# Spare TensorE matmuls on constants inside its waits, and latent sums behind a weight chunk, in a two-block transformer kernel

## The chip, the cores and the metric

One core of a Trainium2 chip runs the whole program. The metric is the device time of one execution in microseconds, lower is better. Engines are named as the profile names them: PE is TensorE's matmuls, PEld its weight loads, DVE VectorE, ACT ScalarE, POOL GpSimd and SP SyncE.

## What is computed

512 tokens of width 1024, all in 32-bit floats, go through two transformer blocks. The first has three branches (windowed attention, a spatial gate, a pooling branch) that are gated and merged, an attention on 256 memory tokens, and a feed-forward layer. The second has two causal attentions over 512 tokens (MLA with a low-rank latent, and "fox" with forget gates) and a layer of experts in which every token takes 16 of 16384 experts in each of 8 heads:

```python
x = x + rmsnorm(merged @ w_out[l], g_norm[l, 1])
ym = memory_attention(rmsnorm(x, g_norm[l, 2]), rmsnorm(mem, g_mem[l]), ...)
x = x + rmsnorm(ym, g_norm[l, 3])
yf = jnp.square(jax.nn.relu(rmsnorm(x, g_norm[l, 4]) @ w_up[l])) @ w_down[l]
x = x + rmsnorm(yf, g_norm[l, 5])
...
h = _modulate(x, norm1_g, shift1, scale1)
cq, ckv, kpe, fq, fk, fv, fl = split(h @ w_in)
q_a = _rms_norm(cq, mla_qa_g) @ w_uq;  kv_a = _rms_norm(ckv, mla_kva_g) @ w_ukv
x = x + gate1 * (concat(attention_a, attention_b) @ w_o)
h2 = _modulate(x, norm2_g, shift2, scale2)
# experts: 16 best of 256 candidate pairs per head; rows of peer_u and peer_v are gathered
a = einsum("bcd,bchkd->bchk", h2, peer_u[e]);  y = einsum("bchk,bchkd->bcd", gate * gelu(a), peer_v[e])
```

## The kernel before

The tokens are done in two halves of 256 (`TH` = 2 tiles of 128; `W` = 256). For each half, `dense(hf)` runs all layers on TensorE, with the activations feature-major: a linear layer is a stream of 128x256 matmuls, eight for each weight chunk of 512 KB. SP loads the chunks in one fixed order into a ring of five; `take` waits for one. Results go to four PSUM banks in turn: `bank()` waits until the result of four banks ago has been emptied (semaphore `lin_evacuated`) and hands out the next one, `lin[0]` counts them.

Each engine has a program of its own, whose order is fixed when the kernel is built. The expert work of half 0 (gathers of `peer_u` rows and dot products on VectorE, then gathers of `peer_v` rows and batches of 16 matmul records in `combine`, L897) is woven into half 1's dense work by a pace that is worked out at build time: `fill()` and `tick()` place the batches that are due by the program's own clock. Half 1's experts come at the end, with nothing dense beside them. In half 0 there is no expert work, and `fill()` places nothing.

Places that the change touches, in the order of a half:

- `attend` (L832): an attention as a pipeline of steps. A step makes the scores of unit i (L846), transposes the probabilities of unit i-2 (L855) and multiplies those of i-3 with the values (L864). The band, memory, mla and fox attentions take 8, 4, 8 and 8 heads by two tiles. At the first head of a tile the output bank must be free (`o_normed` of an earlier group). At a tile's end TensorE waits for the normalised output `o_normed`, transposes it (L872), and the attention ends with a wait for the last copy `pt_copied`. `turned_room` waits until a transposition bank is free. In half 0 other matmuls are put between the steps (gate weights, modulation, fox keys, output weights).
- `sums_of_added` and `sums` (L709, L722): square sums over the features as matmuls against a column of ones (L717, L730), followed by ScalarE's root and VectorE's reciprocal; `spread` (L735) waits for them and spreads the factor over the partitions (L741). `norm` (L744) is both. It is called for the first and second residual norm of half 1 and for the last (`z3`) of both.
- the first norm of the second block: `sums(KB, each=2)`, `spread(True)`, then `linear_fm(hT, 5)` (cq, ckv), a narrow `linear_tok(hT, 1, 40)`, the latent square sums `sums(3)` and `sums(2, first=3)`, then the four chunks of fox values with a `spread()` after the second and the fourth.
- the end of half 0's dense work: `sums(KB, sq=sq_next)` for the next half's first norm, then transposes of h2 (L1210).

## Time and profile before

| | us |
|---|---|
| median of 3 runs (lowest to highest) | 2486.91 (2478.14 to 2488.8) |
| profiled execution, its time | 2490.19 |
| profiled execution, span of its instructions | 2488.4 |
| TensorE busy | 1954.1 (79%) |
| VectorE, ScalarE, GpSimd busy | 1232.9, 503.6, 1098.6 |

### The profile page before, as it was taken

What the parts mean: (1) busy time and instruction counts of PE and PEld (TensorE: products, weight loads), DVE (VectorE), ACT (ScalarE), POOL (GpSimd) and SP (SyncE); (2) the same over time, 40 slices, a digit from 0 to 9 for tenths busy, and PEclk for the clock granted to TensorE, in tenths of its full rate; (3) what the DMA queues carried; (4) which work ended last, traced back from release to release, by engine and by line L of the source; (5) the groups of instructions that cost most, each with busy time, mean ns of one, the idle gap of its engine ahead of it and who ended that gap; (6) DMA issues with size and microseconds to landing.
All of it is one profiled execution on the core that took longest, in us unless ns stands there. A gap on an engine that the chain in (4) does not pass through costs nothing.

```text
span 2488.4 us, 26319 instructions
## 1 busy us (share of the span) xinstructions
PE 1954.1 (79%) x9392; PEld 1363.5 (55%) x9392; DVE 1232.9 (50%) x2969; ACT 503.6 (20%) x1204; POOL 1098.6 (44%) x1090
## 2 busy tenths in 40 slices
PE   8999999999989989998999999887933333333334
PEld 6888778887557767776777764553810000000001
DVE  5455120002425876547634447664667666666540
ACT  3411331101442232124211022442110000000000
POOL 2010000000001556455555554675577777777764
PEclk9999999998989999999999989799956566556557
DMA  7486324443416999999999998899999999999997
GB/s 282 170 318 252 123 94 153 153 152 102 145 55 237 396 354 385 394 405 356 393 389 405 388 360 334 308 353 368 352 362 411 409 409 409 409 410 409 409 409 315
DMA packets 214996, 780.06 MB, mean 313 GB/s; under 512 B 23923, under 2 KB 26547, under 8 KB 213843
## 3 DMA queue, kind: packets, MB, share of 16 engines
q0 software_dynamic: 155120, 564.84, 58.2%
q1 hardware_dynamic: 57560, 208.49, 23.2%
q10 hardware_dynamic: 2187, 5.05, 0.6%
q8 instruction: 76, 1.25, 0.2%
q14 instruction: 53, 0.43, 0.1%
HBM read 771.70 MB, written 6.58 MB: 313 GB/s over the span
## 4 chain that ended last, share of the span: by engine, by line
PE 64%; DMA 14%; POOL 10%; issue 5%; DVE 4%; ACT 3%; ACTq 0%; SPq 0%; POOLq 0%; DVEq 0%
PE bank L648 50%; POOL main L581 8%; DMA main<-in_peer_v,idx_v 6%; PE bank L912 5%; DMA main<-in_peer_u,idx 5%; DMA ring<-in_peer_u,idx 2%; PE bank L846 2%; PE bank L864 2%; POOL ring L581 1%; PE bank L855 1%; ACT main L1259 1%; DMA ring<-in_w_stream 1%; PE bank L730 1%; DVE main L1901 1%; PE bank L1227 1%
## 5 line engine op out<-in xcount | busy, mean ns | idle before, releaser
L648 PE MATMUL bank<-main,ring 128*128 128x256 f32 x4864 | 1078.9, 383 | 10.1 <-ACT main L1477 5.0
L648 PEld LDWEIGHTS bank<-main,ring 128*128 128x128 f32 x4864 | 923.3, 191 | 166.3 <-issue 34.1
L912 PE MATMUL bank<-main,w_wide 128*32 128x512 f32 x2048 | 354.0, 825 | 430.6 <-DMA main<-in_peer_v,idx_v 419.6
L581 POOL DMA_INDIRECT main<-in_peer_v,idx_v x512 | 525.2, 1026 | 371.6 <-PE bank L912 230.6
L581 POOL DMA_INDIRECT main<-in_peer_u,idx x427 | 456.0, 1068 | 268.2 <-issue 116.6
L912 PEld LDWEIGHTS bank<-main,w_wide 128*32 128x32 f32 x2048 | 71.6, 134 | 650.5 <-issue 649.5
L1901 DVE CUSTOM_DVE_ANT_0 main<-h_a,main 128x1024 f32<-128x1024 f32 x256 | 311.4, 1220 | 114.0 <-DMA main<-in_peer_u,idx 101.8
L1259 ACT ACTIVATE main<-bank 128x256 f32<-128x256 f32 (+3 forms) x304 | 125.0, 420 | 700.4 <-PE bank L648 681.4
L648 PE MATMUL bank<-ring,main 128*128 128x512 f32 (+3 forms) x624 | 238.2, 535 | 7.3 <-DMA ring<-in_w_stream 7.3
L1901 DVE CUSTOM_DVE_ANT_0 main<-bank,main 128x1024 f32<-128x1024 f32 x144 | 175.0, 1216 | 122.7 <-DMA main<-in_peer_u,idx 121.5
L648 PEld LDWEIGHTS bank<-ring,main 128*128 128x128 f32 x624 | 108.8, 195 | 109.7 <-issue 95.4
L576 POOL DMA_DIRECT2D main<-in_norm_g x1 | 0.5, 527 | 355.0 <-ACT small L1279 355.0
L1901 DVE CUSTOM_DVE_ANT_0 ring<-bank,ring 128x1024 f32<-128x1024 f32 x80 | 97.2, 1215 | 94.0 <-DMA ring<-in_peer_u,idx 93.5
L574 POOL DMA_DIRECT2D main<-in_w_ada x48 | 25.3, 528 | 190.3 <-DVE main L1757 190.3
L1721 DVE TENSOR_TENSOR main<-main 128x256 f32<-128x256 f32 x36 | 15.3, 424 | 181.0 <-ACT main L1469 180.9
L846 PE MATMUL bank<-main 128*128 128x256 f32 (+9 forms) x224 | 85.9, 471 | 13.6 <-ACT main L1338 7.9
L864 PE MATMUL bank<-main 128*128 128x64 f32 (+1 forms) x496 | 80.8, 296 | 19.0 <-ACT main L1352 11.5
L581 POOL DMA_INDIRECT ring<-in_peer_u,idx x85 | 80.1, 943 | 25.9 <-issue 24.1
L864 PEld LDWEIGHTS bank<-main 128*128 128x128 f32 x496 | 73.2, 215 | 27.1 <-ACT main L1352 21.8
L1374 ACT ACTIVATE dots<-dots 128x32 f32<-128x32 f32 x16 | 3.7, 229 | 415.0 <-DVE dots L1901 415.0
L1338 ACT ACTIVATE main<-bank,small 128x256 f32<-128x256 f32 (+3 forms) x112 | 57.1, 510 | 140.4 <-DVE small L1783 85.8
L1469 ACT ACTIVATE main<-bank 128x256 f32<-128x256 f32 x48 | 18.4, 383 | 279.7 <-PE bank L648 279.7
(247 smaller groups left out, 1512.0 us busy)
## 6 DMA issues: line engine op xcount, KB each, us to landing
ring<-in_w_stream SPq DMA_DIRECT2D x372, 512.0 KB, 6.2
main<-in_w_ada POOLq DMA_DIRECT2D x48, 512.0 KB, 9.7
main<-in_peer_v,idx_v POOLq DMA_INDIRECT x512, 11.3
main<-in_peer_u,idx POOLq DMA_INDIRECT x427, 10.6
main<-in_sub_keys SPq DMA_DIRECT2D x2, 1024.0 KB, 9.8
main<-rows_d SPq DMA_DIRECT2D x1, 1536.0 KB, 10.5
ring<-in_peer_u,idx POOLq DMA_INDIRECT x85, 17.2
main<-in_xT ACTq DMA_DIRECT2D x1, 1024.0 KB, 5.3
```

Of the source, the lines that this page charges most:

```text
L574: gp.dma_start(ada_ring[:, p % ADA_RING, :], T["w_ada"][k * P:(k + 1) * P, s * D:(s + 1) * D]).then_inc(ada_landed[p % ADA_RING], 16)
L581: gp.indirect_dma_start(rows_buf[slot], None, table, bass.IndirectOffsetOnAxis(ap=where, axis=0)).then_inc(landed[slot], 16)
L648: ins = pe.matmul(o, lhsT, rhs, **kw)
L730: last = mm(b[:, t:t + 1], sq[:, first + k, t * P:(t + 1) * P], ones[:, 0:1], start=k == 0 and t == 0, stop=k == nb - 1, skip_group_check= ...
L846: mm(s_bank[u % 2][:, 0:nk], q_of(x), k_of(x, b0 * P, nk), start=True, stop=True).then_inc(S["s_ready"], 1)
L855: last = pe.transpose(pt_bank[x["r"] % 2][:, j * P:(j + 1) * P], probs[:, u % 3, j * P:(j + 1) * P], ident)
L864: last = mm(o_bank(x)[:, x["h"] * dv:(x["h"] + 1) * dv], probsT[:, u % 2, j * P:(j + 1) * P], v_of(x, kb_), start=j == 0, stop=j == len(x[ ...
L912: last = mm(y_bank[half][s * CG:(s + 1) * CG, :], w_wide[:, lo:lo + CG], v_buf[slot][:, half * 512:(half + 1) * 512], start=q == 0, stop=q ...
L1227: last = mm(b[:, p * P:(p + 1) * P], qpT[:, (2 * h + p) % KB, t * P:(t + 1) * P], sub_keys[:, 2 * h + p, :], start=True, stop=True)
L1259: ac.activation(dst, s, func, **kw).then_inc(S["lin_evacuated"], 1)
L1338: ac.activation(probs[:, u % 3, 0:nk], s_bank[u % 2][:, 0:nk], ACT.Exp, scale=neg_r[:, x["tl"]:x["tl"] + 1] if kind == "mem" else -1.0, bi ...
L1901: st.begin(ve.tensor_tensor_reduce(out=u_buf[slot], in0=h2, in1=u_buf[slot], scale=1.0, scalar=0.0, op0=ALU.mult, op1=ALU.add, accum_out=d ...
```

## The change

`keep_busy(n, bank)` issues n matmuls of the identity with 256 constant columns into a PSUM bank that is free at that time; nothing reads the result. `keep_busy_dense(n)` does so in the bank that `bank()` would give next, after the same wait. They are called:

- in `sums_of_added` ahead of the wait for the squares (1, in `norm`), in `sums` for every second block (1), in `spread(True)` ahead of the wait for the factor (2) and behind it (4 in `norm`, 2 in the second block's norm), the last two only where `fill()` places no expert batch; `fill()` now returns whether it did;
- in `attend` behind the second scores if no batch was placed there (3), ahead of the wait for the output bank at the second tile's first head where both tiles use the same bank (3), ahead of the wait for the last normalised output (2, with `turned_room` moved in front), and ahead of the last copy (1);
- at half 0's h2: 1 for every second of eight blocks of the sums, and 3 behind them.

The latent sums are moved behind the first of the four fox value chunks; their two banks and the two of the values are taken ahead of that chunk.

```diff
--- before.py
+++ after.py
@@ -629,6 +629,7 @@
             lin = [0]
             clock = [0.0]
             experts_now = [None]
+            batches = [0]
 
             mm = pe.matmul
 
@@ -641,8 +642,21 @@
 
             def fill():
 
+                placed = batches[0]
                 if experts_now[0] is not None:
                     experts_now[0].until(clock[0] + EARLY)
+                return batches[0] > placed
+
+            def keep_busy(n, idle_bank):
+
+                for _ in range(n):
+                    mm(idle_bank[:, 0:W], ident, cst[:, 0:W], start=True, stop=True)
+
+            def keep_busy_dense(n):
+
+                if n and lin[0] > 3:
+                    pe.wait_ge(S["lin_evacuated"], lin[0] - 3)
+                keep_busy(n, psum[lin[0] % 4])
 
             def mmw(o, lhsT, rhs, **kw):
                 ins = pe.matmul(o, lhsT, rhs, **kw)
@@ -706,9 +720,10 @@
             norms = [0]
             sq_seen = [0]
 
-            def sums_of_added(hf, name, b=None):
+            def sums_of_added(hf, name, b=None, busy=0):
 
                 b = bank() if b is None else b
+                keep_busy(busy, b)
                 n, other = (KB, KB - 1) if name[0] == "z" else (KB // 2, 1)
                 pe.wait_ge(S["sq_ready"], SQUARES[hf][name] + n)
                 pe.wait_ge(S["sq_added"], ADDED[hf, name])
@@ -719,12 +734,14 @@
                 sq_seen[0] += n
                 results(last)
 
-            def sums(nb, first=0, sq=sqT, b=None, each=1):
+            def sums(nb, first=0, sq=sqT, b=None, each=1, busy=0):
 
                 b = bank() if b is None else b
                 for k in range(nb):
                     if k % each == 0:
                         sq_seen[0] += 1
+                    if k % 2 == 0:
+                        keep_busy_dense(busy)
                     pe.wait_ge(S["sq_ready"], sq_seen[0])
                     for t in range(TH):
                         last = mm(b[:, t:t + 1], sq[:, first + k, t * P:(t + 1) * P], ones[:, 0:1],
@@ -734,8 +751,8 @@
             def spread(may_fill=False, r=rstd):
 
                 norms[0] += 1
-                if may_fill:
-                    fill()
+                if may_fill and not fill():
+                    keep_busy_dense(2)
                 pe.wait_ge(S["rstd_ready"], norms[0])
                 for t in range(TH):
                     last = mm(rbc[:, t * P:(t + 1) * P], r[:, t:t + 1].to_broadcast([P, P]), ident, start=True, stop=True)
@@ -743,10 +760,11 @@
 
             def norm(hf, name):
 
-                sums_of_added(hf, name)
+                sums_of_added(hf, name, busy=1)
                 spread(True)
                 clock[0] += 6.0
-                fill()
+                if not fill():
+                    keep_busy_dense(4)
 
             def mod_row(s):
 
@@ -844,8 +862,9 @@
                             pe.wait_ge(S["p_ready"], u - 1)
                         b0, nk = x["blocks"][0], len(x["blocks"]) * P
                         mm(s_bank[u % 2][:, 0:nk], q_of(x), k_of(x, b0 * P, nk), start=True, stop=True).then_inc(S["s_ready"], 1)
-                        if i == 1:
-                            fill()
+                        if i == 1 and not fill():
+                            turned_room(units[0]["r"])
+                            keep_busy(3, pt_bank[units[0]["r"] % 2])
                     if 2 <= i <= n + 1:
                         x = units[i - 2]
                         u = x["u"]
@@ -859,6 +878,8 @@
                         u = x["u"]
                         pe.wait_ge(S["pt_copied"], x["r"] + 1)
                         if x["h"] == 0 and x["g_prev"] is not None:
+                            if x["tl"] and not x["other"]:
+                                keep_busy(3, pt_bank[x["r"] % 2])
                             pe.wait_ge(S["o_normed"], x["g_prev"] + 1)
                         for j, kb_ in enumerate(x["blocks"]):
                             last = mm(o_bank(x)[:, x["h"] * dv:(x["h"] + 1) * dv], probsT[:, u % 2, j * P:(j + 1) * P],
@@ -866,15 +887,20 @@
                         last.then_inc(S["av_done"], 1)
                     if i in ends:
                         x = ends[i]
+                        turned_room(x["ro"])
+                        if i == max(ends):
+                            keep_busy(2, pt_bank[x["ro"] % 2])
                         pe.wait_ge(S["o_normed"], x["g"] + 1)
-                        turned_room(x["ro"])
                         for j in range(4):
                             last = pe.transpose(pt_bank[x["ro"] % 2][:, j * P:(j + 1) * P], o_tok[:, j * P:(j + 1) * P], ident)
                         last.then_inc(S["pt_ready"], 1)
                     while early is not None and early_done < by_step(total, steps, i):
                         early_done = next(early)
                     tick(each)
-                pe.wait_ge(S["pt_copied"], ends[max(ends)]["ro"] + 1)
+                last_ro = ends[max(ends)]["ro"]
+                pe.wait_ge(S["pt_copied"], last_ro)
+                keep_busy(1, pt_bank[(last_ro + 1) % 2])
+                pe.wait_ge(S["pt_copied"], last_ro + 1)
 
             def turn_idx(k):
 
@@ -896,6 +922,7 @@
 
             def combine(b):
 
+                batches[0] += 1
                 for s in range(N_CG):
                     slot, fills = v_slot(N_CG * b + s)
                     pe.wait_ge(v_landed[slot], 16 * (fills + 1))
@@ -1059,17 +1086,20 @@
                     results(last)
                 mark("norm3")
                 norm(hf, "z3")
-                sums(KB, each=2)
+                sums(KB, each=2, busy=1)
                 spread(True)
                 clock[0] += 6.0
-                fill()
+                if not fill():
+                    keep_busy_dense(2)
                 mark("cq")
                 linear_fm(hT, 5, first_wait=h_block)
                 linear_tok(hT, 1, 40)
-                sums(3)
-                sums(2, first=3)
+                q_sums, kv_sums = bank(), bank()
                 banks = [bank() for _ in range(TH)]
-                tok_chunks(banks, hT, 0, 2, 4, 512)
+                tok_chunks(banks, hT, 0, 1, 4, 512)
+                sums(3, b=q_sums)
+                sums(2, first=3, b=kv_sums)
+                tok_chunks(banks, hT, 1, 2, 4, 512)
                 spread()
                 results(tok_chunks(banks, hT, 2, 4, 4, 512), TH)
                 spread()
@@ -1199,7 +1229,8 @@
                         tick(7.1)
                 mark("h2")
                 if hf == 0:
-                    sums(KB, sq=sq_next)
+                    sums(KB, sq=sq_next, busy=1)
+                    keep_busy_dense(3)
                 clock[0] += 6.0
                 fill()
                 for t in range(TH):
```

## Rows read from the trace of the kernel before

**Rows 1.** The page's granted clock in tenths, in 40 equal slices of 62 us.
```profile
PEclk9999999998989999999999989799956566556557
```

**Rows 2.** Stages: from:to length, busy PE PEld DVE ACT POOL, clock, DMA share, GB/s.
```profile
0.00:815.00 815.00, 773.01 (x3498) 625.41 (x3499) 253.91 (x574) 222.60 (x561) 49.54 (x79) 0.96 0.50 173
815.00:1445.00 630.00, 608.23 (x3111) 475.33 (x3110) 371.53 (x934) 138.26 (x348) 358.94 (x322) 0.99 0.99 387
1445.00:1740.00 295.00, 262.49 (x1263) 154.44 (x1263) 178.32 (x396) 99.27 (x209) 168.75 (x150) 0.90 0.91 343
...
1815.00:2488.40 673.40, 240.20 (x1132) 52.83 (x1132) 383.10 (x926) 25.83 (x45) 482.74 (x504) 0.61 1.00 397
```

**Rows 3.** Stretches of low granted clock, same columns.
```profile
113.10:116.50 3.40, 3.27 (x15) 3.27 (x16) 1.42 (x4) 1.15 (x4) 0.00 (x0) 0.50 0.01 2
...
300.90:314.50 13.60, 13.60 (x55) 12.17 (x55) 2.70 (x10) 5.13 (x16) 0.00 (x0) 0.50 0.00 1
...
573.90:587.60 13.70, 11.24 (x43) 10.36 (x44) 8.19 (x17) 6.21 (x13) 0.53 (x1) 0.50 0.17 52
608.10:614.90 6.80, 6.80 (x17) 4.13 (x17) 0.17 (x1) 0.52 (x2) 0.00 (x0) 0.50 0.22 69
693.40:703.60 10.20, 8.32 (x37) 6.98 (x38) 2.65 (x5) 4.98 (x9) 0.00 (x0) 0.50 0.00 0
...
741.20:744.60 3.40, 3.40 (x15) 2.99 (x14) 0.00 (x0) 2.29 (x4) 0.20 (x1) 0.50 0.02 4
765.10:775.30 10.20, 6.94 (x26) 5.89 (x25) 5.70 (x12) 3.76 (x8) 0.00 (x0) 0.50 0.06 9
...
1126.90:1130.30 3.40, 3.39 (x8) 2.76 (x9) 3.23 (x6) 3.37 (x8) 1.37 (x2) 0.50 1.03 410
...
1488.70:1492.10 3.40, 3.40 (x6) 1.32 (x5) 0.00 (x0) 1.32 (x2) 0.07 (x1) 0.50 1.03 410
1574.00:1594.50 20.50, 20.50 (x74) 13.42 (x74) 10.75 (x30) 6.42 (x18) 12.16 (x11) 0.50 0.90 332
1601.30:1611.60 10.30, 9.72 (x34) 7.47 (x35) 3.97 (x12) 2.75 (x8) 1.68 (x2) 0.50 0.63 232
```

**Rows 4.** PE's timeline, waits in brackets: start, busy, line, tiles, form, count.
```profile
111.89 0.66 PE L872 MATMUL bank<-cst,main 128*128 128x128 f32 x4 [1.28 <-DVE main L1797]
...
299.43 0.61 PE L788 MATMUL bank<-ones,main 128*128 128x1 f32 x4 [1.96 <-ACT gate L1299]
...
574.46 6.96 PE L730 MATMUL bank<-ones,main 128*128 128x1 f32 x32 [2.33 <-ACT main L1478]
...
582.04 1.22 PE L741 MATMUL bank<-cst,small 128*128 128x128 f32 x4 [0.62 <-DVE small L1697]
...
710.05 0.49 PE L846 MATMUL bank<-main 66*128 66x128 f32 x2 [2.02 <-ACT main L1338]
...
1601.88 1.94 PE L864 MATMUL bank<-main 128*128 128x64 f32 x8 [2.15 <-DVE main L1797]
```

**Rows 5.** The chain that ended last: start, length, engine, line, records.
```profile
805.23 6.91 PE bank L648 x32
...
1590.68 3.57 PE bank L912 x16
...
1612.44 1.85 PE bank L912 x16
```

**Rows 6.** PE's timeline where a spare would meet little or no wait.
```profile
76.72 1.46 PE L648 MATMUL bank<-main,ring 128*128 128x256 f32 x6
...
1186.49 0.71 PE L741 MATMUL bank<-cst,small 128*128 128x128 f32 x4 [0.55 <-DVE small L1697]
...
1624.88 0.66 PE L872 MATMUL bank<-cst,main 128*128 128x128 f32 x4
```

**Rows 7.** PE's waits 1560 to 1740 us (total, times, longest), and a POOL timeline row.
```profile
PE bank L912 <- DMA main<-in_peer_v,idx_v: 17.1, 6, 5.5
...
1612.98 1.25 POOL L581 DMA_INDIRECT main<-in_peer_u,idx  x1 [8.38 <-DVE dots L1901]
```

## The prediction

> **What bounds the kernel now.** I read the granted clock of the page first, then the busy time by stage, then TensorE's timeline around each place where the clock is low, then the waits of the gathers. The clock line [rows 1] is at or near full for most slices and dips at a few of the first 29. Every dip that I enlarged is a stretch at 0.50 exactly, which is the 1.2 GHz level against 2.4 GHz. By stage [rows 2], tokens of half 0 (0 to 815 us) and half 1 (815 to 1740) keep TensorE busy 95%, 97% and 89% of the time: there TensorE is the bound. From 1815 us on it is 36% busy and the DMA engines are full at 397 GB/s: that end is a queue of gathered expert rows, its length set by bytes. It starts when the routing of half 1 is through, so a microsecond saved before about 1740 us should be a microsecond off the end. TensorE's slow clock in the end stretch costs nothing.
>
> The mean clocks of the first three stages (0.96, 0.99, 0.90) mean 2 x (0.04 x 815 + 0.01 x 630 + 0.10 x 295) = 137 us at half speed before 1740 us. At most half of that, 68 us, can come back, and only where TensorE is what the stretch waits for. This is the ceiling.
>
> **What precedes a dip.** It is waiting of one or two microseconds, not long idleness: the end of the first attention (1.28 us for the normalised output) is followed by 1.2 GHz, so are the head of the memory attention (1.96), the fox head (2.02) and the last norm of the first block (2.33) [rows 4]. The length of the low stretch is out of proportion to the wait: 13.6 us after 1.96 [rows 3].
>
> **Price of a spare.** 32 records, which are 16 matmuls of 128x256, take 6.91 us [rows 5]: 0.43 us for one. An expert batch takes 1.85 us at 2.4 GHz and 3.57 at 1.2 [rows 5], so a spare that runs at the low level is 0.83.
>
> **Part 1, spares at the ends of attentions** (two ahead of the wait for the normalised output, one ahead of the last copy). 0.86 us lies in waits like the 1.28 of the first attention; hidden. Four stretches of 3.4 us in half 0 hang on an end or on the fox head; the first and the last of them have TensorE busy 3.27 and 3.40 us [rows 3]. That is dense work at half speed, so about 1.6 each; at the fox head each unit also waits for ScalarE, so I take 1.4 as the mean: **5.6 us**. The mla end (10.2 us low, 8.3 busy [rows 3]) begins ahead of the spares; they can only bring the clock back sooner. Between 0 and 3; I take 1.5.
>
> **Part 2, three spares at the heads**, 1.3 us, placed only if no expert batch was placed there. In the memory attention of half 0 they fit the wait of 1.96 [rows 4]. The 13.6 us behind it are wholly TensorE-busy [rows 3], on many small matmuls that cannot bring the clock back by themselves. Half of it is 6.8; I take **6.5**. In half 0's band attention the next matmuls follow the scores without a wait [rows 6], because chunks of gate weights are put there: three spares are 1.3 us on the path. The mla head has such fillers too; I charge both in full: **-2.6**.
>
> **Part 3, three spares ahead of the second tile's first output**, which must wait for the normalisation of the first tile (same PSUM bank): 1.3 in the 2.15 us of half 1's mla attention [rows 4]. The 10.3 us low behind it are 9.7 busy [rows 3]: **5.0**.
>
> **Part 4, the last norm of the first block and its square sums.** One spare, two, then four and one more in the waits up to 2.33 [rows 4]: hidden. In half 0 13.7 us are low with 11.2 busy [rows 3], but VectorE's and ScalarE's chain hides part of it. Of the sums, 8 records of one column for each pair of blocks run in the low stretch, and with the clock up TensorE no longer trails the squares. Against it stand four spares between the pairs, and two behind in a wait of 0.62 [rows 4], 0.24 too short for them. If the clock falls during the sums all the same, those spares cost double. Bounds -3 and +3.5; I take **2** because the first wait is well filled.
>
> **Part 5, latent sums behind one chunk of weights.** Single-column sums right behind a narrow matmul are followed by 6.8 us low, all busy [rows 3]: half, 3.4, is the most. But all four banks are now taken ahead of the chunk, so TensorE first waits until ScalarE has emptied the last narrow results, and the narrow matmul is itself light work, so the fall may come anyway. 0 to 3.4; **1.5**. SP's weight queue keeps its order; no DMA is moved. The sums end one chunk later, and one chunk instead of two stands between them and their use.
>
> **Part 6, h2 of half 0**: seven spares (3.0 us) around sums that run without a wait, ahead of transposes that wait for VectorE; 10.2 us low with 6.9 busy [rows 3]. Hidden only because the second tile's rows come late. If not hidden, -3; **2.1** taken: the dense part of the stretch at half price.
>
> Half 0: 5.6 + 1.5 + 6.5 - 2.6 + 2 + 1.5 + 2.1 = 16.6 us.
>
> **Half 1.** The same sites gain less, as expert batches fill or occupy the waits. Four low stretches at norms and latent sums, the first and last 3.4 us [rows 3], together 3.1: there VectorE and ScalarE pace the blocks. The mla second tile: 5.0. Exposed spares: two behind a batch at the mla end, where the transposes now follow at once [rows 6], two likewise at the band end, three at the second norm against a wait of 0.55 [rows 6], one at the fox end: 0.86 + 0.86 + 0.74 + 0.43 = 2.9. Net 5.2. The largest stretch, 20.5 us low and wholly busy at 1574 [rows 3], is not in the sum: a batch is placed at that head, so no spare is.
>
> **Sum**: 16.6 + 5.2 = 21.8 us. The profiled execution took 2490.2 us, 3.3 above the median of 2486.9; the slow stretches differ from run to run as waits fall differently, so I subtract from the median: **2465 us**. 0.5% (12.4 us) is about what a measurement of this kernel can tell from no change.
>
> **A rule against it.** The Trainium skill (TensorE: Matmul & The Clock Gate, Why this matters for your kernels) warns of idle gaps between bursts of matmuls that are longer than any wait filled here. By it these waits would not lower the clock, and the spares could give nothing. The trace disagrees in the four places of [rows 4] named above. The rival that it makes is the second below.
>
> **Rivals.**
> *The mla head of half 1 stays fast too.* It began after several short waits, and its matmuls then held a pace at 1.2 GHz that never brought the clock back. A small shift in what precedes could spare it. About 7.5 of 20.5 us, as at full clock the units are bound by VectorE and ScalarE: 2457. For: the start moves. Against: no spare is put there. 0.20.
> *Spares do not move the clock.* The waits are a symptom, and the light work around them (transposes, single columns) is what lowers it. Then only exposed spares count: 2.6 + 2.9, some 6 us: 2493. Against: dense work ends each low stretch. 0.08.
> *Half 1's gain is taken back by gathers.* TensorE already waits 17.1 us for value rows between 1560 and 1740 us [rows 7]; a faster TensorE asks for them sooner. For: these waits. Against: GpSimd itself sat 8.4 us waiting for a VectorE dot just ahead of that [rows 7], and that dot is held up by the slow stretch at 1601. Half 0's gain alone: 2470. 0.12.
> *The dips move.* Waits that stay unfilled, such as those ahead of the mla attentions, catch the clock where they missed it before, and half the gain goes: 2476. 0.09.
> *Slower: spares at the low level.* Where the clock has fallen before the spares, they run at 0.83 each and push the awaited transposes and sums back. If they restored it nowhere: about 0.7 for each of eight attention ends (three spares are 2.5 us there, of which I estimate that waits like the 1.28 [rows 4] hide two thirds), 4 for the sums of each half's last norm, 1 for h2 beyond its wait, with 2.6 + 2.9 doubled: 5.6 + 8 + 1 + 11 = 26 us, less waits that hide a third: about 18: 2505. It decides against the kernel from the point where over half the sites are already low when the spares start. For: the mla end and the band end of half 1. Against: elsewhere the wait itself is the first lapse. 0.06.
>
> **How the numbers follow.** Forecast 0.45, with 2456 to 2474 of its own from parts 4 to 6. The range leaves out the second and last rival and a tail of the first: 2447 to 2483. Faster by over 0.5% (below 2474.5): forecast 0.44, first rival 0.20, third 0.09, fourth 0.04, so 0.77. Slower (above 2499.3): 0.05. Within: 0.18.
>
> **What would show it.** Right: the granted clock at 1.00 through the memory attention of half 0, at both its ends and at the second mla tile of half 1; TensorE's waits there filled by the new matmul line; batches and the end queue unchanged in length. Wrong: low stretches of the same length after filled waits (second rival); longer waits of TensorE for value rows between 1560 and 1740 (third); a spare line with a mean near twice 0.43 us and waits gone ahead of it (last); or low clock at 655 to 660 us or around 900, where it was full before (fourth).

## The result, and the profile after

The median of 18 executions went from 2491.04 to 2477.82 us; the ratio is 0.9946 (95% interval 0.9927 to 0.9965), some 13.4 us less. The forecast was 21.8 us less. So the time fell, as forecast, and lies within the range, by about three fifths of the expected amount. The kernel before came out 4.1 us above the 2486.91 that the forecast started from; the rest of the distance from 2465 to 2477.8 is a gain that was forecast too large. The profiled execution took 2483.59 us, 5.8 above the median (its span 2481.8), which matters below: it holds a long stretch at 1.2 GHz that some other profiles lack.

The granted clock on the page of after, beside [rows 1]:

```profile
PEclk9999999998999999999999999979965566565556
```

Stages of after (from:to length, busy time and records of PE, PEld, DVE, ACT, POOL, granted clock, DMA share, GB/s). In order: half 0's memory attention with its output layer; half 0's last norm of the first block to the end of the fox values; the same of half 1; half 1's mla attention; its fox attention; the end stretch.

```profile
295.10:331.10 36.00, 33.58 (x184) 27.49 (x185) 8.96 (x26) 16.62 (x46) 0.00 (x0) 1.00 0.19 59
562.40:650.00 87.60, 86.63 (x321) 56.27 (x321) 33.02 (x80) 26.33 (x52) 0.53 (x1) 0.90 0.36 118
...
1440.00:1546.10 106.10, 103.64 (x442) 58.45 (x443) 70.33 (x161) 30.42 (x58) 48.23 (x46) 1.00 0.93 351
1554.20:1605.30 51.10, 46.04 (x285) 29.25 (x286) 43.73 (x111) 22.90 (x55) 41.12 (x33) 0.97 0.99 368
1605.30:1675.60 70.30, 64.92 (x338) 42.40 (x339) 36.82 (x79) 26.30 (x62) 41.07 (x39) 0.76 0.81 291
1797.70:2481.80 684.10, 252.24 (x1171) 54.89 (x1169) 388.10 (x942) 31.40 (x54) 489.72 (x508) 0.58 1.00 395
```

The memory attention is now wholly at 2.4 GHz. The fox attention of half 1 is at 0.76, where before it was at 0.94 and the mla attention at 0.76: the long low stretch of half 1 [rows 3, the one at 1574] has not gone; in this profile it stands one attention later. The end stretch is as long as it was (682.3 before, 684.1 now, both from the last key score to the end of the span), so of the 8.4 us that the dense part gains in these two profiles all but 1.8 reach the end.

The same stages in both kernels and in four experiments told below, in us, each from its first matmul to the next stage's first; in brackets the us at 1.2 GHz, where there are any, summed from the granted clock (0.3 us and less, and the end, are left out):

| stage | before | after | no spares | half 0 spares | half 1 spares | first units |
|---|---|---|---|---|---|---|
| half 0 band attention | 37.9 | 39.2 | 38.0 | 39.2 | 38.0 | 37.9 |
| to the memory attention | 181.4 (3.3) | 179.8 | 181.4 (3.4) | 179.8 | 181.3 (3.1) | 179.8 |
| half 0 memory attention | 43.2 (17.1) | 36.0 | 40.4 (10.2) | 36.0 | 44.9 (20.5) | 36.0 |
| half 0 last norm to fox values | 86.3 (20.5) | 87.6 (17.1) | 85.4 (17.1) | 84.5 (10.2) | 84.6 (17.1) | 85.9 (13.7) |
| half 0 mla attention | 35.4 (6.3) | 35.6 (3.1) | 35.5 (2.4) | 35.2 | 35.5 (6.5) | 35.6 (3.1) |
| half 0 fox attention | 41.1 (7.4) | 39.8 (3.7) | 44.6 (14.6) | 38.9 | 41.1 (7.2) | 39.8 (3.7) |
| half 0 output layer, h2 | 40.8 (13.6) | 39.4 (3.4) | 40.9 (13.6) | 39.2 (6.8) | 40.7 (13.7) | 39.5 (3.4) |
| half 1 mla attention | 63.2 (30.7) | 51.0 (3.4) | 54.0 (10.2) | 51.9 (6.8) | 50.9 (3.4) | 50.0 |
| half 1 fox attention | 56.6 (6.8) | 70.4 (34.1) | 67.6 (30.7) | 58.2 (6.8) | 70.1 (34.1) | 56.2 |
| last key score to last matmul | 675.9 | 677.3 | 675.5 | 675.6 | 677.7 | 675.8 |

The waits that were filled, in TensorE's timeline of after (start, busy, line, tiles, form, count, wait ahead): the end of the first attention, the head of the memory attention, and the fox head of half 0, as three of [rows 4]. L653 is a spare, L895 the transposes of a finished output, L806 the woven modulation.

```profile
112.45 1.08 PE L653 MATMUL bank<-cst 128*128 128x256 f32 x4
113.90 0.66 PE L895 MATMUL bank<-cst,main 128*128 128x128 f32 x4 [0.36 <-DVE main L1828]
...
297.75 1.46 PE L653 MATMUL bank<-cst 128*128 128x256 f32 x6
299.87 0.61 PE L806 MATMUL bank<-ones,main 128*128 128x1 f32 x4 [0.66 <-ACT gate L1330]
...
700.13 0.71 PE L864 MATMUL bank<-main 66*128 66x128 f32 x4 [1.67 <-ACT main L1290]
700.68 1.80 PE L653 MATMUL bank<-cst 128*128 128x256 f32 x6
```

The wait of 1.28 is 0.36 now, that of 1.96 is 0.66. At the fox head the spares stand behind the scores, while the wait is ahead of them: 1.67 of 2.02 us is left, and 3.7 us stay at the low level in that attention.

### The profile page after: what moved, and what is told of

The parts are those of the page before. It is cut to its first block, busy times and chain, and to the rows that moved or that the text cites. A ratio compares the mean times of both kernels' runs of the same rounds, so it can differ in the third digit from the quotient of the medians.

```text
span 2481.8 us, 26696 instructions
## 1 busy us (share of the span) xinstructions
PE 1983.9 (80%) x9588; PEld 1374.1 (55%) x9588; DVE 1231.7 (50%) x2969; ACT 503.2 (20%) x1204; POOL 1098.7 (44%) x1090
## 3 DMA queue, kind: packets, MB, share of 16 engines
q8 instruction: 78, 1.28, 0.2%
## 4 chain that ended last, share of the span: by engine, by line
PE 60%; DMA 15%; POOL 12%; issue 6%; DVE 4%; ACT 3%; SPq 0%; POOLq 0%; DVEq 0%; ACTq 0%
PE bank L662 48%; POOL main L581 11%; DMA main<-in_peer_v,idx_v 5%; DMA main<-in_peer_u,idx 5%; PE bank L939 4%; DMA ring<-in_peer_u,idx 3%; PE bank L864 2%; PE bank L885 1%; POOL ring L581 1%; PE bank L653 1%; DVE main L1932 1%; DMA ring<-in_w_stream 1%; ACT main L1290 1%; PE bank L874 1%; PE bank L1258 1%
## 5 line engine op out<-in xcount | busy, mean ns | idle before, releaser
L939 PE MATMUL bank<-main,w_wide 128*32 128x512 f32 x2048 | 361.7, 841 | 425.8 <-DMA main<-in_peer_v,idx_v 414.8
L939 PEld LDWEIGHTS bank<-main,w_wide 128*32 128x32 f32 x2048 | 72.1, 135 | 651.8 <-issue 650.6
L885 PE MATMUL bank<-main 128*128 128x64 f32 (+1 forms) x496 | 77.2, 286 | 13.2 <-ACT main L1383 12.6
L864 PE MATMUL bank<-main 128*128 128x256 f32 (+9 forms) x224 | 82.1, 452 | 6.7 <-ACT main L1290 5.0
L1369 ACT ACTIVATE main<-bank,small 128x256 f32<-128x256 f32 (+3 forms) x112 | 57.2, 511 | 137.5 <-DVE small L1814 87.6
L885 PEld LDWEIGHTS bank<-main 128*128 128x128 f32 x496 | 69.2, 204 | 22.7 <-ACT main L1383 19.9
L1814 DVE CUSTOM_DVE_ANT_0 bank<-bank,cst 128x128 f32<-128x128 f32 (+3 forms) x64 | 31.9, 498 | 86.8 <-PE bank L864 86.7
## 6 DMA issues: line engine op xcount, KB each, us to landing
main<-in_peer_u,idx POOLq DMA_INDIRECT x427, 10.3
```

What stands on the lines that cost most here:

```text
L864: mm(s_bank[u % 2][:, 0:nk], q_of(x), k_of(x, b0 * P, nk), start=True, stop=True).then_inc(S["s_ready"], 1)
L885: last = mm(o_bank(x)[:, x["h"] * dv:(x["h"] + 1) * dv], probsT[:, u % 2, j * P:(j + 1) * P], v_of(x, kb_), start=j == 0, stop=j == len(x[ ...
L939: last = mm(y_bank[half][s * CG:(s + 1) * CG, :], w_wide[:, lo:lo + CG], v_buf[slot][:, half * 512:(half + 1) * 512], start=q == 0, stop=q ...
L1369: ac.activation(probs[:, u % 3, 0:nk], s_bank[u % 2][:, 0:nk], ACT.Exp, scale=neg_r[:, x["tl"]:x["tl"] + 1] if kind == "mem" else -1.0, bi ...
L1814: st(ve.tensor_tensor_reduce(out=s[:, 0:nk], in0=s[:, 0:nk], in1=causal, scale=1.0, scalar=3.0e38, op0=ALU.add, op1=ALU.min, accum_out=low ...
```

## The experiments

The theory: a short wait of TensorE is followed by a stretch at 1.2 GHz, and spare work in the wait prevents it. The rivals: the clock does not follow the spares; the gain is handed back to the experts' gathers; half 1's long stretch comes and goes by itself.

**Spares without columns.** All spares keep their places and count, but stream one column instead of 256.

```diff
-mm(idle_bank[:, 0:W], ident, cst[:, 0:W], start=True, stop=True)
+mm(idle_bank[:, 0:1], ident, cst[:, 0:1], start=True, stop=True)
```

> The changed kernel with every spare cut from 256 columns to one: same count, places and waits, nearly no work in them. If the spares act by the work that they give TensorE (my theory), the granted clock falls again at the head of half 0's memory attention, some 13 us at 0.50, and the time is that of the kernel before, ratio 0.999 to 1.003. If it is enough that TensorE issues something in the wait, or if the gain came from the moved waits and the moved sums, the ratio stays near 0.9946.

Measured: 2497.66 us, ratio 1.0038 (1.0018 to 1.0058). The memory attention of half 0 in a window (columns as above):

```profile
295.70:335.70 40.00, 36.47 (x185) 31.25 (x184) 8.96 (x26) 16.73 (x45) 0.00 (x0) 0.87 0.17 53
```

and in TensorE's timeline:

```profile
298.93 0.72 PE L653 MATMUL bank<-cst 128*128 128x1 f32 x6
301.05 0.61 PE L806 MATMUL bank<-ones,main 128*128 128x1 f32 x4 [1.39 <-ACT gate L1330]
```

A wait of 1.39 us is left, and the clock falls (0.87; 36.0 us and 1.00 in after). The time is a little above the range that was expected for this theory. So the work in the spares carries the whole gain. It doesn't tell whether it is the columns or the time that they fill: the light spares do less of both. This kernel's ratio is above that of one without spares (below), though their intervals overlap; its profiled execution was its fastest (2484.98 us) and shows little of it, so whether it is slower, and why, is open.

**Spares in the batch's wait at two heads of half 1.** In after, a head at which an expert batch is placed gets no spares, even where TensorE then waits inside the batch for value rows. Here 4 (mla) and 10 (fox) spares stand ahead of that wait.

```diff
+HEAD_SPARES = {"mla": 4, "fox": 10}
...
+if i == 1 and hf and kind in HEAD_SPARES:
+    turned_room(units[0]["r"])
+    head_busy[0] = (HEAD_SPARES[kind], pt_bank[units[0]["r"] % 2])
...
 batches[0] += 1
+if head_busy[0] is not None:
+    keep_busy(*head_busy[0])
+    head_busy[0] = None
```

> The changed kernel with spares also in half 1's wait for value rows at the heads of the mla attention (4) and the fox attention (10), between the expert weights' turn and the batch. Theory: the changed kernel's 34 us at 0.50 in half 1's fox attention follow from that unfilled wait; filled, the stretch stays at 1.00, fox is some 13 us shorter than in the changed kernel's profile, and the median gains 4 to 10 us more, ratio to before 0.990 to 0.993. Rival: the gathers set the pace there, so TensorE waits longer for value rows later and the ratio stays at 0.9946.

Measured: 2475.74 us, ratio 0.9949 (0.9928 to 0.9969), no different from after. But its two attentions, mla and fox, are at full clock from end to end, the first kernel of which that is true; their windows:

```profile
1553.70:1604.50 50.80, 46.46 (x292) 30.56 (x292) 43.59 (x111) 22.92 (x55) 40.87 (x33) 1.00 1.00 369
1604.50:1659.80 55.30, 54.20 (x359) 37.15 (x360) 36.64 (x79) 26.31 (x62) 44.19 (x37) 1.00 0.96 351
```

and its fox head in TensorE's timeline (L654 spares, L950 a batch):

```profile
1611.75 4.48 PE L654 MATMUL bank<-cst 128*128 128x256 f32 x20
1616.64 1.92 PE L950 MATMUL bank<-main,w_wide 128*32 128x512 f32 x16 [0.41 <-DMA main<-in_peer_v,idx_v]
```

The two attentions take 106.1 us, against 121.4 in after. The expected ratio (0.990 to 0.993) didn't come: the median doesn't show what the profile shows. So what one profile shows here is probably not what every execution does. The later kernels take this up.

**The latent sums back in front.**

```diff
-q_sums, kv_sums = bank(), bank()
-banks = [bank() for _ in range(TH)]
-tok_chunks(banks, hT, 0, 1, 4, 512)
-sums(3, b=q_sums)
-sums(2, first=3, b=kv_sums)
-tok_chunks(banks, hT, 1, 2, 4, 512)
+sums(3)
+sums(2, first=3)
+banks = [bank() for _ in range(TH)]
+tok_chunks(banks, hT, 0, 2, 4, 512)
```

> The changed kernel with the latent sums back in front of the fox value chunks. In the profiles the stretch from the narrow matmul to the turn of the mla keys took 54.2 us after the change against 52.1 before. If the move costs, the ratio falls to 0.993 to 0.9945 and one wait of about 0.6 us ahead of the first value chunk goes; if it gains as I forecast (1.5 us in half 0, less in half 1), the ratio rises to 0.9955.

Measured: 2479.91 us, ratio 0.9976 (0.9954 to 0.9998), in the same comparison as the heads kernel. The intervals overlap, so the move's own worth isn't settled, though the ratio lies on the side on which the move gains, above the 0.9955 expected of that. In half 0 the stage from the last norm to the fox values is 85.4 us here and 81.7 to 87.6 in the eight profiles with both the move and half 0's spares there.

**Three spares at one head alone**, that of half 0's memory attention, in the kernel before.

```diff
 if i == 1:
     fill()
+    if kind == "mem" and not hf:
+        turned_room(units[0]["r"])
+        for _ in range(3):
+            mm(pt_bank[units[0]["r"] % 2][:, 0:W], ident, cst[:, 0:W], start=True, stop=True)
```

> The kernel before with one part alone: three spares behind the second scores of half 0's memory attention. Theory: the low stretch of 13.6 us there is gone, the stage from its first score to the second norm's sums is 36 instead of 43 us, and the time falls by 5 to 7 us, ratio 0.997 to 0.998. Rival: half 1 gives it back at its waits for expert rows, ratio 1.000 with the stage shorter all the same.

Measured: 2478.23 us, ratio 0.9983 (0.9958 to 1.0008). The median can't tell 4 us from nothing; the stage can:

```profile
295.40:331.40 36.00, 32.30 (x178) 26.61 (x178) 8.96 (x26) 16.57 (x46) 0.00 (x0) 1.00 0.18 59
```

43.2 us became 36.0, and the 17.1 us at 1.2 GHz are gone, for 1.3 us of spares. One wait of 1.96 us was the cause of all of it, the 3.4 us at the end of that attention (321.3 to 324.7 us in the kernel before) included, where this kernel has no spare. It is no chance of one profile: the stage takes 36.0 or 36.1 us, without low clock, in all ten profiles that have these spares, and 40.0 to 44.9 in the four that have none or light ones. The rule that the prediction weighed (the Trainium skill, TensorE: Matmul & The Clock Gate, Why this matters for your kernels), that the gaps which cost are longer ones, does not hold here: an edit shows it, not only the order in time.

**The moves without spares** (`keep_busy` issues nothing), **the spares of half 0 only, those of half 1 only, and all of them once more**, beside one another on one chip. In the first three the latent sums are where after has them.

```diff
 def keep_busy(n, idle_bank):
-    for _ in range(n):
-        mm(idle_bank[:, 0:W], ident, cst[:, 0:W], start=True, stop=True)
+    if experts_now[0] is None:      # half 0 only; "is not None": half 1 only; no spares: pass
+        for _ in range(n):
+            mm(idle_bank[:, 0:W], ident, cst[:, 0:W], start=True, stop=True)
```

> The changed kernel without any spare: only the latent sums behind the first value chunk and the waits that were moved forward are left. If the spares carry the whole gain, the ratio to before is 0.999 to 1.002. If the moved parts cost something of their own, as the run with one-column spares suggests (1.0038), it is 1.002 to 1.004. If the latent move gains by itself, 0.997 to 0.999.

> The changed kernel with the spares of half 0 alone, the moves kept in both halves. By my sum half 0 carries 16.6 of 21.8 us, so about three quarters of the gain: ratio 0.995 to 0.9965. If the exposed spares of half 1 eat what the others win there, it equals the whole change, 0.9946, or is better.

> The changed kernel with the spares of half 1 alone, the moves kept. By my sum 5 us, ratio 0.998 to 0.999. If half 1's gain is given back at the waits for value rows, or its exposed spares eat it, 1.000 to 1.002 (as e5_no_spares).

> The changed kernel itself, on the same chip as the three parts: 0.9946 again. Its profile shows whether the 34 us at 0.50 in half 1's fox attention come back: if they follow from that head's wait for value rows in every execution, they are there again; if it is chance how the waits fall, this profile is without them.

| spares | median us | ratio | interval |
|---|---|---|---|
| none | 2490.44 | 1.0004 | 0.9980 to 1.0028 |
| half 0 | 2478.95 | 0.9970 | 0.9946 to 0.9995 |
| half 1 | 2490.06 | 1.0017 | 0.9997 to 1.0038 |
| both | 2477.49 | 0.9961 | 0.9941 to 0.9981 |

The last row is after itself, which gave 0.9946 in the first comparison: a gain of 10 us here, of 13 there. As far as these intervals tell, the whole gain is half 0's. Half 1's spares give nothing that can be measured, and the moves alone nothing; the 0.998 to 0.999 that was expected of half 1 lies outside its interval. In the profile of half 1's spares the long stretch stands in the fox attention, as in after and in the kernel with no spares; with all spares a second time it stands in the mla attention, as in before. So which of the two attentions has the stretch in after is hardly an effect of the change.

**What holds the stretch.** TensorE's timeline of after at half 1's fox head (L939 is an expert batch of 16 records, L864 scores, L874 transposes, L885 the products with the values):

```profile
1608.95 1.92 PE L939 MATMUL bank<-main,w_wide 128*32 128x512 f32 x16
...
1617.86 3.64 PE L939 MATMUL bank<-main,w_wide 128*32 128x512 f32 x16 [5.22 <-DMA main<-in_peer_v,idx_v]
...
1629.81 1.59 PE L864 MATMUL bank<-main 66*128 66x384 f32 x2
1631.19 0.85 PE L874 MATMUL bank<-cst,main 128*128 128x128 f32 x3
1631.83 1.38 PE L885 MATMUL bank<-main 128*128 128x64 f32 x6
...
1646.80 3.64 PE L939 MATMUL bank<-main,w_wide 128*32 128x512 f32 x16
...
1651.41 0.60 PE L874 MATMUL bank<-cst,main 128*128 128x128 f32 x4
```

It begins with a wait of 5.22 us for value rows. Then each unit takes 3.2 us (1629.81 to 1633.01) and TensorE is busy all through, without leaving 1.2 GHz. The first dense work is the batch at 1646.80, and behind it the clock is full (transposes of four blocks in 0.60, of three in 0.85 ahead of it). In every profile with such a stretch and without a burst in it (before, after, no spares, half 1 spares, both again, lean) it ends with an experts' batch, or less than 1 us behind one. Three kernels test this.

**A burst.** After, with eight spares once in the eighth unit of half 1's mla and fox attention.

```diff
 turned_room(x["r"])
+if hf and kind in ("mla", "fox") and i == 7:
+    keep_busy(8, pt_bank[x["r"] % 2])
```

> The changed kernel with 8 more spares, once, in the eighth unit of half 1's mla and once of its fox attention. If the long low stretch of these attentions holds itself there, because their thin matmuls don't win the clock back once it has fallen, the burst ends it: no low stretch behind the eighth unit, at most some 15 us of low clock in either attention, and executions that lie closer together; it costs 3.4 us each (8 by 0.43) where the clock was full already, and saves up to 8 where it wasn't, so a ratio of 0.992 to 0.996. If the stretch comes from something outside TensorE, it runs past the burst (24 to 34 us of low clock in one of them), and the burst only costs: ratio 0.996 to 0.999.

Measured: 2481.46 us, ratio 0.9972 (0.9950 to 0.9993). Its long stretch was in the fox attention again; TensorE's timeline there (L653 spares, L864 scores, L876 transposes, L887 products):

```profile
1635.30 0.85 PE L876 MATMUL bank<-cst,main 128*128 128x128 f32 x3
1635.94 1.38 PE L887 MATMUL bank<-main 128*128 128x64 f32 x6
1637.11 1.59 PE L864 MATMUL bank<-main 66*128 66x384 f32 x2
1638.50 5.24 PE L653 MATMUL bank<-cst 128*128 128x256 f32 x16
1643.57 0.49 PE L876 MATMUL bank<-cst,main 128*128 128x128 f32 x3
1643.90 0.78 PE L887 MATMUL bank<-main 128*128 128x64 f32 x6
```

The same instructions take 0.85 and 1.38 ahead of the burst, 0.49 and 0.78 behind it: the clock comes back 3.3 us into the spares, where the units ahead of them had stayed low. Other thin work did win it back elsewhere: in the kernel before the low stretch that ends at 703.6 [rows 3] ends within a row of 32 transposes that began at 699.67. As an edit the burst doesn't pay: 20.6 us at 1.2 GHz had gone ahead of it and 3.3 more went in it, the fox attention is 69.5 us against 70.4, and the burst in the mla attention, where the clock was full, made it 53.6 instead of 51.0. The stretch ended in the burst, as expected of one that holds itself; the expected price (0.992 to 0.996) did not come out. The ratio lies where the rival, a cause outside TensorE, had it (0.996 to 0.999), but by that rival the stretch would have run past the burst.

**A lean kernel.** After, with the spares inside the two heads, and without those that its trace shows in full on the path (half 0's band head; the ends of half 1's band, mla and fox attention).

```diff
 if i == 1 and not placed:
     turned_room(units[0]["r"])
-    keep_busy(3, pt_bank[units[0]["r"] % 2])
+    if hf or kind != "band":
+        keep_busy(3, pt_bank[units[0]["r"] % 2])
...
-if i == max(ends):
+if i == max(ends) and (not hf or kind == "mem"):
     keep_busy(2, pt_bank[x["ro"] % 2])
...
-keep_busy(1, pt_bank[(last_ro + 1) % 2])
+if not hf or kind == "mem":
+    keep_busy(1, pt_bank[(last_ro + 1) % 2])
```

> The changed kernel, less the spares that its trace shows in full on the path (three at the head of half 0's band, and those at the ends of half 1's band, mla and fox attention, where an experts' batch stands ahead of them), and with 4 and 10 spares inside the batch's wait for its value rows at the heads of half 1's mla and fox attention. The theory that spares pay where they keep the clock and cost their own duration where nothing waits: band of half 0 back to 37.9 us (-1.3), band, mla and fox ends of half 1 each 1 to 2 us shorter, no long low stretch at either head; some 4 us below the changed kernel at least, ratio to the kernel before 0.990 to 0.993. The rival, that what half 1's dense work gains is given back to the experts' transfers: ratio 0.994 to 0.996, as the changed kernel.

> Both edits of the two kernels beside it. If the filled waits at the two heads already keep the clock, the bursts only cost: 6.8 us above the lean kernel, ratio 0.993 to 0.996. If the low stretch still comes back in part of the lean kernel's executions, the bursts save there what they cost elsewhere, and the two are within 2 us, with executions that lie closer together here.

Measured: lean 2473.96 us, ratio 0.9942 (0.9921 to 0.9962); with bursts too, 2474.21, 0.9957 (0.9936 to 0.9978). The lean kernel misses the expected 0.990 to 0.993; the two lie within 2 us of one another, as was expected if the stretch still comes back. The fox attention is at full clock in both profiles, as in the heads kernel, but the mla attention has the long stretch (20.5 and 17.1 us), although its head was filled. The lean kernel's window of the mla attention, and in TensorE's timeline the beginning and end of the stretch (L865 scores, L892 products with the values, L952 a batch):

```profile
1550.50:1609.10 58.60, 54.19 (x287) 35.55 (x288) 43.22 (x111) 22.88 (x55) 38.69 (x33) 0.83 0.88 321
```

```profile
1556.89 0.91 PE L865 MATMUL bank<-main 96*128 96x384 f32 x2 [0.59 <-ACT main L1382]
...
1559.26 0.91 PE L865 MATMUL bank<-main 96*128 96x384 f32 x2 [1.13 <-ACT main L1382]
...
1560.82 0.88 PE L892 MATMUL bank<-main 128*128 128x64 f32 x6 [0.32 <-ACT main L1396]
1561.54 1.51 PE L865 MATMUL bank<-main 96*128 96x384 f32 x2
1562.84 0.85 PE L881 MATMUL bank<-cst,main 128*128 128x128 f32 x3
...
1578.02 3.64 PE L952 MATMUL bank<-main,w_wide 128*32 128x512 f32 x16
```

It follows three waits of 0.59, 1.13 and 0.32 us for ScalarE in the first units, which no spare fills. Over all 14 profiles, two waits of 0.59 to 1.64 us, ahead of the third and the fourth score, stand in exactly the four that have the long stretch in the mla attention (before, both again, lean, lean with bursts). The heads kernel has one (1.10), the other nine none above 0.3. In eight of these nine the batch at that head waits 2.3 to 3.1 us for its rows; in the four it waits 1.6 us or less. So in this attention the long stretch goes with the shorter wait at the head, and filling that head alone left the next two waits open. In the kernel with bursts the eight spares stand at 1569.60, and the low stretch ends in them, at about 1572.

**The first units filled.** The lean kernel with two spares ahead of the third and two ahead of the fourth score of half 1's mla attention.

```diff
 if i < n:
     x = units[i]
     u = x["u"]
+    if hf and kind == "mla" and i in (2, 3):
+        keep_busy(2, pt_bank[units[i - 2]["r"] % 2])
     if u >= 2:
         pe.wait_ge(S["p_ready"], u - 1)
```

> The lean kernel with two more spares ahead of the third and two ahead of the fourth score of half 1's mla attention, where the traces show TensorE waiting 0.6 to 1.24 us for ScalarE's probabilities. If the long low stretch there (20.5 us in the lean kernel's profile, from its third unit on) begins in these short waits, it is gone: at most 6.8 us of low clock in the mla attention, 51 to 53 us instead of 58.5, a ratio of 0.990 to 0.993. If waits that short play no part, the stretch is there as before (17 us or more of low clock), and the ratio is that of the lean kernel or up to 0.0005 above it, 0.994 to 0.995. The four spares cost at most 1.7 us.

Measured: 2467.49 us, ratio 0.9932 (0.9905 to 0.9959), with six executions from 2464.54 to 2475.63. Its window of the mla attention, and its first units in TensorE's timeline (L654 spares, L867 scores):

```profile
1555.10:1605.10 50.00, 47.06 (x295) 30.76 (x296) 42.88 (x111) 22.84 (x55) 40.24 (x33) 1.00 1.00 368
```

```profile
1560.10 1.13 PE L654 MATMUL bank<-cst 128*128 128x256 f32 x4
1561.41 0.91 PE L867 MATMUL bank<-main 96*128 96x384 f32 x2 [0.18 <-ACT main L1384]
...
1562.49 1.03 PE L654 MATMUL bank<-cst 128*128 128x256 f32 x4
1563.78 0.91 PE L867 MATMUL bank<-main 96*128 96x384 f32 x2 [0.27 <-ACT main L1384]
```

The mla attention has no low clock at all, better than expected (nor has the fox attention, as in the lean kernel). This is one profile, and nine others lack the stretch without these spares, so by itself it could be chance. The nearest kernel to compare is the lean one with bursts: its head batch starts as early (3.2 us behind the first score in both), its two waits are 1.24 and 1.13 instead of 0.18 and 0.27, and it has the stretch. This is the fastest of the kernels by its median and its ratio; its interval overlaps that of the lean kernel, so its lead over the lean kernel rests on the windows, and over the kernel before on the ratio.

## Why the prediction was right in its direction and too large

**The bound, and that it is dense time that counts: right.** From the last key score to the last matmul all the profiles take 675.3 to 677.7 us, whatever happened ahead of it. The rival by which gathers take the gain back is wrong in after: TensorE's waits for value rows between 1550 and 1740 us are

```profile
PE bank L939 <- DMA main<-in_peer_v,idx_v: 17.9, 6, 5.2
```

against 17.1 in 6 [rows 7].

**The clock follows short waits, and spares hold it: right in the attentions, not at the sums.** The rival "spares do not move the clock" falls with the memory head and the light spares, but what it says of light work holds in part: at the last norm of half 0 the clock falls at 571.9 us, where TensorE has had no wait that the timeline shows for seven us and alternates single-column sums with spares. Half 0's time up to half 1's first band score is 901.1, 903.5, 903.0 and 901.7 us in the four profiles whose half 0 has no spares or light ones (before, light, none, half 1), a mean of 902.3, and 893.4, 891.5, 891.0, 889.8, 889.6 and 891.5 in six with all of them (after, heads, latent back, half 0, both again, burst), a mean of 891.1. That is 11.2 us, for which the prediction had 16.6. By the same kernels, stage by stage (the stages do not part the prediction's terms exactly):

- Part 2, memory head: 43.2, 40.0, 40.4 and 44.9, in the mean 42.1, became 36.0: 6.1; forecast 6.5. **Right**, as part of the sum below.
- Part 1 with the fox head: the stretch behind the band attention 181.4 to 179.8, the fox attention 42.6 to 39.3 in the mean, 4.9 together; forecast 5.6. But of the four stretches in that term the memory attention's end belongs to the memory stage, where the head's spares alone remove it, and the fox attention's end to part 6's stage; and a part of the mla end's stretch lies in the fox stage. So compare parts 1, 2 and 6 together: 15.7 forecast (5.6 + 1.5 + 6.5 + 2.1), 12.8 measured. **Right in kind, some 3 too large.** The fox head might give more if its spares stood ahead of the wait.
- The band head: 38.1 to 39.2 in the mean, 1.1 lost; 1.3 was charged. **Right**; the lean kernel is back at 37.9. The mla attention, whose head was charged 1.3 too (its end's 1.5 is counted above): 35.8 in the mean either way.
- Part 6: 40.9 to 39.1 in the mean, 1.8; forecast 2.1, and part 1's fox end is in it.
- Parts 4 and 5, forecast 2 and 1.5: **wrong**. The stage from the last norm to the fox values has a mean of 85.9 us with the spares and 85.6 without, 0.3 lost. With the three lean profiles, which have the same spares here (81.8, 81.7 and 85.9), and the memory head's (87.1, none here) it is 85.0 and 85.9, 0.9 gained: next to nothing either way. The step that failed is "hidden", with its reason that the first wait is well filled: the clock fell without a wait, and the hedge behind it came true. TensorE's timeline of after:

```profile
570.54 1.05 PE L747 MATMUL bank<-ones,main 128*128 128x1 f32 x8
571.46 0.73 PE L653 MATMUL bank<-cst 128*128 128x256 f32 x2
571.99 1.86 PE L747 MATMUL bank<-ones,main 128*128 128x1 f32 x8
573.71 2.05 PE L653 MATMUL bank<-cst 128*128 128x256 f32 x4
575.56 1.06 PE L758 MATMUL bank<-cst,small 128*128 128x128 f32 x4
...
595.78 3.71 PE L662 MATMUL bank<-ring,main 128*128 128x40 f32 x32
600.11 6.64 PE L662 MATMUL bank<-ring,main 128*128 128x512 f32 x8 [0.62 <-ACT small L1290]
```

  The clock falls amid the single-column sums although a spare stands between every eight of them (1.05 for a group, then 1.86), and from there on a spare costs 1.0 instead of 0.43 (four records, two spares, in 2.05). VectorE has the factor at 574.42 (its reciprocal starts at 574.25 and takes 0.17 us), but the two spares hold TensorE until 575.56: 1.1 us late. At the latent sums the fall comes at 599.3, as the narrow 128x40 matmuls end and just ahead of the wait of 0.62, before the moved sums are reached, as the lower bound of part 5 said.

In sum 6.1 + 4.9 - 1.1 + 1.8 - 0.3 = 11.4, the rest being the scatter of stages that the change doesn't touch. Of the 5.4 us that are missing, 3.8 are parts 4 and 5 by these profiles.

**Half 1: 5.2 forecast, nothing measured** (1.0017 for its spares alone). The norms and the latent sums less the exposed spares at the band end and the second norm were +1.5 in the sum. Half 1 without its mla and fox attentions takes a mean of 784.9 us in the six profiles with its spares (782.8 after, 786.6 heads, 789.5 latent back, 783.5 half 1, 783.1 both again, 783.6 burst) and 786.3 in four without or with light ones (785.3 before, 787.1 light, 785.7 memory head, 786.9 none): 1.4. A fifth without, half 0's spares alone, takes 795.6 with 30.7 us low at its last norm and is left out of that mean; with it the difference is 3.2. The three lean profiles, which lack only the spares at the band's end, take 789.6, 783.5 and 790.5; with them nearly nothing or some 2 us are left. So the sign may be right, but profiles that scatter by 8 us don't settle the size. The exposed spares were where they were forecast, the first at double price; in TensorE's timeline of after, the ends of half 1's band and mla attention:

```profile
928.37 3.64 PE L939 MATMUL bank<-main,w_wide 128*32 128x512 f32 x16
931.94 2.01 PE L653 MATMUL bank<-cst 128*128 128x256 f32 x4
...
1601.15 1.92 PE L939 MATMUL bank<-main,w_wide 128*32 128x512 f32 x16
1603.01 1.13 PE L653 MATMUL bank<-cst 128*128 128x256 f32 x4
```

The second tile of the mla attention (part 3) was the mis-sized term: 5.0 forecast less 0.86 for its end, 4.1. Where no long stretch is in it, that attention takes 54.0, 51.8, 54.0 and 51.9 us without these spares (light, memory head, none, half 0) and 51.0, 50.8, 50.8 and 50.9 with them (after, heads, latent back, half 1): 2.0 net. The 10.3 us that I read [rows 3] were the longest case: in the profiles without spares there are 3.4 to 6.8 us low at that place (10.2 in before).

What hid this, and made the sum's half 1 worthless for a forecast, is the long stretch. The prediction left it out of the sum and gave it to the first rival as a chance (20.5 us low, worth 7.5). The place was right, and so was the reading: that it follows several short waits is what the waits in all 14 profiles bear out, and "its matmuls then held a pace at 1.2 GHz that never brought the clock back" is what the burst confirms. What it missed is that the stretch has other places: the head of the fox attention, where a batch stands and no spare is placed either, and in the kernel with no spares that attention's second tile, behind a wait of 1.54 us. The mla and fox attentions together take 114.4 to 123.1 us (mean 119.7) in the eight profiles with a long stretch in one of them (17 us or more), and 106.1 to 110.3 (mean 108.4) in the six without: 11 us. Which of the two has it, or neither, changes from one kernel to the next with and without spares. That is more than a third of the spread between executions of the kernel before (2475.13 to 2504.37), and twice the 5.2 that I added up there.

**Against after's own profile** the sum is 8.4 us at the last key score (1806.1 to 1797.7), of which 7.7 come from half 0 and 0.8 from half 1, where 12.2 gained in the mla attention are lost as 13.8 in the fox attention.

**The slower rival** (spares at the low level) holds in after's profile at three sites, the last norm (1.0 us for a spare), half 0's mla end (1.06) and half 1's band end (1.0), all of which it named, not at the half of the sites from which it would decide.

**Open**: whether and why the light spares are slower than none; what the latent move is worth by itself; in what share of a kernel's executions the long stretch stands, since only profiled ones show it; and why, of the ten profiles without spares in the fox head's wait, three stayed low after it: in these the clock fell 0.9 to 1.5 us ahead of the batch, in the seven others 2.3 to 3.9, but no run tests whether that decides it.

## What to carry to other kernels

Enlarge the granted clock around every short wait of TensorE, and price a filler by the stage it stands in, for here it paid only ahead of work that stayed at 1.2 GHz without it; put it inside the wait, not behind it, and not where the clock has fallen before the filler starts. A low stretch that sustains itself belongs in a forecast as a chance with a price in every place where it can start, not as the one place where a single profile shows it. If medians differ by less than the spread of executions, compare the one stage that the edit touches across all the profiles.

## What the hardware showed beyond expectation

- Thin work at 1.2 GHz stayed there though TensorE was busy all through: seven attention units in a row at 3.1 to 3.8 us in after (1623.51 to 1646.80), against 1.9 us for a unit at 2.4 GHz in the burst kernel. A batch of 3.4 to 3.6 us, or 2.5 to 3.3 us of spares, ended such a stretch each time.
- Waits of 0.59, 1.13 and 0.32 us in a row, with thin matmuls between them, stood ahead of one (lean); with 0.18 and 0.27 left of the waits there was none (first units, one profile).
- The clock also fell with no wait at all: amid single-column sums with a spare between every eight records of them (571.9 us in after).
- Equal waits don't have equal consequences. In the ten profiles without spares in the wait of half 1's fox head, TensorE waits 3.89 to 6.49 us there for value rows, and runs the batch behind it wholly or mostly at 1.2 GHz (3.35 to 3.64 us). In seven of them the low stretch is 6.8 us, in three (after, half 1 spares, burst) the same batch does not end it and it lasts 23.9 to 34.1. With ten spares in that wait 0.41 to 1.87 us of it are left, and the clock stays full in all four.
